# A decoder layer on one core: the second norm's modulation rows, two at a time inside attention

## The chip, the core and the metric

The kernel runs on one NeuronCore of a Trainium2 chip. The core has five engines that run their own instruction streams and meet only at semaphores: TensorE (PE; its weight loads are PEld), VectorE (DVE), ScalarE (ACT), GpSimd (POOL) and SyncE (SP), which here only issues DMAs. The metric is the device time of one execution in microseconds.

## The reference, cut to what matters

```python
mod = silu(c) @ w_ada + b_ada                        # c: 1 x 1024, w_ada: 1024 x 6144
shift1, scale1, gate1, shift2, scale2, gate2 = split(mod, 6)
h    = rms_norm(x, norm1_g) * (1 + scale1) + shift1  # x: 512 x 1024
q, k, v, qi, ki, wi, u, g_attn, g_pool = split(h @ w_in)
attn = top-128 attention (8 heads of 64; the keys by an indexer from qi, ki, wi)
pool = pooled means of u, a 128 x 128 product per group, a scale
x    = x + gate1 * ((sigmoid(g_attn) * (attn @ w_attn_br)
                     + sigmoid(g_pool) * (pool @ w_pool_br)) @ w_out)
h2   = rms_norm(x, norm2_g) * (1 + scale2) + shift2
x    = x + gate2 * ((silu(a) * b) @ w_down)           # a, b: a causal conv of h2 @ w_up
```

The change is about `shift2` and `scale2`, parts 3 and 4 of `mod` (part 1 is `scale1`, part 2 `gate1`, part 5 `gate2`). They are used for the first time in the second norm, long after attention.

## The kernel before, in words

Activations lie with their channels on the 128 partitions and the 512 tokens along the free dimension. Every float32 product is made of three passes over rounded parts: ACT copies 128 x 1024 weights out of `stage` into `wsplit` as the high part (line 732), POOL subtracts to get the low part (line 650), and PE multiplies the high part with both parts of the activations (line 1471, 16 matmuls, "high products") and the low part with the high part of the activations (line 1480, 8 matmuls, "low products"). `wsplit` has three places; ACT prepares weights three units ahead of PE.

**Loads.** SP issues everything in one fixed order. A weight item goes to one of three places of `stage`; it is issued when POOL has made the last low part from what lay there (`load_item`, line 539). ACT waits for the item's semaphore before it copies, and whatever stands behind that copy in ACT's stream waits too.

**One part of `mod` on DVE and PE.** For parts 1 to 5, DVE multiplies eight rows of 128 x 1024 by one column of `silu(c)` each and adds them into an accumulator (`mod_row_of`: the first row line 1091, the other seven line 1094); each row reads the sum that the row before it left. PE then adds up the partitions with eight products whose output is one column each (`mod_columns`, line 1565, 16 matmul records), and DVE adds the bias (`mod_vector`, line 1108). For parts 3 and 4 the rows come in four loads of 1 MB each (`load_early`), into `ada_early`, with accumulators of their own (`macc_early`). DVE adds part 3 behind the first norm and part 4 between the q products; PE's column sums stand behind `squares(3)` and behind the pooling product `u1`, in the bank PT.

**Attention** is 32 steps and five more to drain, written out step by step for each engine (t is the step; a pair is an even step and the odd one after it). At an even t PE computes the scores of steps t and t+1 (line 1707), then at each t the transposes of step t-3 (line 1719), and one half of a filler product: at even t its high products, at odd t its low ones, and at odd t behind them the products with v (line 1741). The fillers are listed in `FILLERS`: gp2, gp3, pb0, pb1, gp4, gp5, pb2, pb3, gp6, gp7, pb4 to pb7, ga0 to ga3. They share two banks in turn, so a filler may start when the filler two before it has been drained: a gp by ACT's tanh (line 847), a pb by DVE (line 1331). In each step DVE adds the scores to the ALiBi terms and takes their maximum (line 1309), makes the bias (line 1313), and normalises the probabilities of the step before (line 1320). ACT makes the ALiBi terms (line 889), exponentiates (line 920), copies the transposed probabilities (line 928) and, after a filler's low half, calls `chunk(name)`: it waits for the filler's product, copies the high part of the weights three units on, and only then drains the bank:

```python
def pool_gate(m):
    chunk(("gp", m))
    me.did(act.activation(ypool[:, m, :], bank(("gp", m))[:, :], ACT.Tanh, scale=0.5), drained["act"])
```

So the copy of gp4's weights stands in ACT's stream right ahead of the tanh that drains gp3, and pb1, two fillers on from gp3, waits for that tanh.

Of the kernel before, what the change touches and what calls it, by code (L numbers as in the profile page):

```python
# [11 lines left out]
P = 128  # L12
# [201 lines left out]
def build_layer(nc, x, c, w_ada, b_ada, norm1_g, w_in, q_norm_g, k_norm_g, w_attn_br, w_pool_grp, pool_scale,  # L214
# [17 lines left out]
    with ExitStack() as ctx:  # L232
# [102 lines left out]
        ada_early = [arena(f"ada_early{n}", [P, 2, D], F32, (24, 36, 44, 52)[n]) for n in range(KD // 2)]  # L335
        macc_early = [arena(f"macc_early{n}", [P, D], F32, (16, 20)[n]) for n in range(2)]
# [18 lines left out]
        def column_bank(j):  # L355

            return {1: OB, 4: PT[1]}.get(j, PT[0])
# [7 lines left out]
        ada_early_in = [sem(f"ada_early_in{q}") for q in range(KD // 2)]  # L365
# [169 lines left out]
        def _(sp):  # L535
# [52 lines left out]
            def load_early(j, q):  # L588
                sp.wait_ge(mod_sum, KD if j == 3 else KD * ROW_TURN[3] + 2 * q + 2)
                if j == 3 and q == 0:  # L590
                    sp.wait_ge(mod_first, 1)
                sp.dma_start(ada_early[q][:, :, :], ada[:, 2 * q:2 * q + 2, j * D:(j + 1) * D]
                             ).then_inc(ada_early_in[q], 16)

            for n, item in enumerate(sch.items):
                if n == NSTAGE:
                    for q in range(KD // 2):
                        load_early(3, q)
                if n in (NSTAGE + 3, NSTAGE + 4):
                    for q in (2 * (n - NSTAGE - 3), 2 * (n - NSTAGE - 3) + 1):  # L600
                        load_early(4, q)
                if item[:3] == ("w", "up", (3 * P, FF + 3 * P)):
                    sp.wait_ge(x2_ok, 2 * NT)
                    sp.dma_start(gate_row[:, :], b_ada[0:1, 5 * D:6 * D].to_broadcast([P, D])).then_inc(gate_in, 16)
                    for q in range(KD // 2):
                        load_last(q)
                load_item(n)
            for n in range(2 * NT):
                half, t = divmod(n, NT)
                sp.wait_ge(out_ok, n + 1)  # L610
                sp.dma_start(out[0, t * P:(t + 1) * P, half * S:(half + 1) * S], ost[:, t, :]).then_inc(stored[t], 16)
# [435 lines left out]
        def _(dve):  # L1047
# [16 lines left out]
            def mod_row_of(j, k):  # L1064

                q, r = divmod(k, 2)
                if j == 1:
                    if r == 0:
                        dve.wait_ge(ada_in[q][j], 16)
                    elif q == KD // 2 - 1:  # L1070
                        dve.wait_ge(ada_end_in, 16)
                    row = ada_first[q][j][:, r, :]
                elif j in (3, 4):
                    if r == 0:
                        dve.wait_ge(ada_early_in[q], 16 * (j - 2))
                    row = ada_early[q][:, r, :]
                elif j == 2:
                    if r == 0:
                        dve.wait_ge(ada_mid_in[q % 2], 16 * (q // 2 + 1))
                    row = ada_mid[q % 2][:, r, :]  # L1080
                else:
                    if r == 0:
                        dve.wait_ge(ada_last_in[q], 16)
                    row = ada_last[q][:, r, :]
                acc = macc_early[j - 3] if j in (3, 4) else macc
                if k == 0:
                    if j == 2:
                        dve.wait_ge(used, sch.unit["mg", KA - 2] + 1)
                    if j == 5:
                        dve.wait_ge(gate_sum, 2)  # L1090
                    me.did(dve.tensor_scalar(acc[:, :], row, csil[:, 0:1], None, ALU.mult), mod_sum)
                else:
                    dve.wait_ge(mod_sum, KD * ROW_TURN[j] + k)
                    me.did(dve.scalar_tensor_tensor(out=acc[:, :], in0=row, scalar=csil[:, k:k + 1],  # L1094
                                                    in1=acc[:, :], op0=ALU.mult, op1=ALU.add), mod_sum)
# [74 lines left out]
            mod_rows(3, 0)  # L1170
            mod_rows(3, 1)
# [7 lines left out]
            mod_rows(3, 2)  # L1179
            mod_rows(3, 3)  # L1180
# [41 lines left out]
            for n in range(KA):  # L1222
# [9 lines left out]
                mod_rows(4, n)  # L1232
# [32 lines left out]
            mod_vector(3)  # L1265
            top_rounds(2)
            pool_mean(1)
            mod_vector(4)
# [65 lines left out]

            def merged_low(m):
# [5 lines left out]
            for m in range(KD):  # L1341
                if m:
                    merged_low(m - 1)
                if m in (2, 4):
# [119 lines left out]
        def _(pe):  # L1464
# [94 lines left out]
            def mod_columns(j):  # L1559
# [3 lines left out]
                acc = macc if j == 1 else macc_early[j - 3]  # L1563
# [5 lines left out]
            def gate_sums(j, n):  # L1569

                pe.wait_ge(mod_sum, KD * (ROW_TURN[j] + 1))
                for half in range(2):
# [68 lines left out]
            def v_turn(m):  # L1641
                pe.wait_ge(drained["act"], drained_count[sch.chunk["v", m]][1])
                if m < 2:
                    pe.wait_ge(mod_ok, ROW_TURN[3 + m] + 2)
# [20 lines left out]
            mod_columns(3)  # L1665
            for g in range(1, KA):
                product(("u", g), hT)
                if g == 1:
                    mod_columns(4)
# [24 lines left out]
            for t in range(SLOTS - 1):  # L1694
# [27 lines left out]
                if filler(t) and t < STEPS + 3:  # L1722
                    name, part = filler(t)
                    if part == "high":
                        await_bank(pe, name)
                    (high_products if part == "high" else low_products)(
                        sch.unit[name], bank(name), mix if name[0] == "pb" else hT)
                if t % 2 and 5 <= t < STEPS + 4:
# [8 lines left out]
                    if (t - 5) % (2 * NT) == 0 and m >= 2:  # L1737
                        pe.wait_ge(head_lo, m - 1)
                    for j in range(i + 1):
# [8 lines left out]
            for m in range(0, KD, 2):  # L1748
                for n in (m, m + 1):
                    product(("ab", n), qT)  # L1750
                if m + 4 < KD:
# [114 lines left out]
```

## Time and profile before

| | us |
|---|---|
| median of three runs | 754.99 (754.11 to 756.42) |
| the profiled execution, its own time | 759.15 |
| its span, first to last instruction | 757.2 |
| PE busy | 739.7 (98% of the span) |
| DVE, ACT, POOL busy | 379.0, 306.6, 312.3 |

PE is busy nearly everywhere; the first norm lies around 39 to 53 us, the u products start near 93 us, attention runs from about 187 to 298 us, the second norm lies near 360 to 400 us, and the MLP fills the rest.
### The profile page before, as it was taken

Reading aid. Unit: us, or ns where it says so; the run is one execution under the profiler, and the core shown is the slowest. Engines: PE = TensorE matmul, PEld = TensorE weight load, DVE = VectorE, ACT = ScalarE, POOL = GpSimd, SP = SyncE. Lnnn points to the kernel's source line nnn. Section 1 sums busy time; section 2 is a strip of 40 time slices with the busy share of each in tenths; the row PEclk is TensorE's granted clock in tenths of the full one; section 3 lists DMA queues with packets and bytes.
Section 4 is the critical chain, followed back from the end, with each engine's and each line's share of the span. In section 5 each row is a group of like instructions: output and inputs, shape, how many; then the busy total and the mean of one; then the engine's idle time right before and its main releaser. Section 6 shows DMA issues by size and latency. Waiting matters only on the chain.

```text
span 757.2 us, 9497 instructions
## 1 busy us (share of the span) xinstructions
PE 739.7 (98%) x3568; PEld 597.2 (79%) x3568; DVE 379.0 (50%) x693; ACT 306.6 (40%) x501; POOL 312.3 (41%) x165
## 2 busy tenths in 40 slices
PE   4989999999999999999999999999999999999997
PEld 3467788888777777887899888888788888888886
DVE  2588699972446551774685435464443433004002
ACT  4224513256756763334455343434334343212120
POOL 1125338562623332547423444444444444443431
PEclk9969989999999999999999999999999999999999
DMA  8995511221113113644338344323323321233301
GB/s 327 381 338 204 187 55 57 71 97 56 57 57 112 57 56 107 262 159 128 97 95 267 112 111 112 91 76 112 101 68 110 111 99 68 84 112 112 137 2 56
DMA packets 83995, 92.75 MB, mean 122 GB/s; under 512 B 2035, under 2 KB 66287, under 8 KB 83951
## 3 DMA queue, kind: packets, MB, share of 16 engines
q1 hardware_dynamic: 82719, 87.43, 35.6%
q10 hardware_dynamic: 1232, 4.72, 1.7%
q8 instruction: 29, 0.48, 0.3%
q14 instruction: 15, 0.12, 0.1%
HBM read 90.05 MB, written 2.10 MB: 122 GB/s over the span
## 4 chain that ended last, share of the span: by engine, by line
PE 96%; DVE 1%; DMA 1%; ACT 1%; SPq 0%; issue 0%; DVEq 0%; ACTq 0%
PE bank L1471 42%; PE bank L1491 21%; PE bank L1480 21%; PE bank L1547 2%; PE bank L1741 1%; PE bank L1719 1%; PE bank L1707 1%; PE bank L1513 1%; PE bank L1625 1%; DMA xtok<-in_x_dram 1%; PE bank L1565 1%; PE bank L1614 1%; ACT junk L747 1%; PE bank L1518 1%; PE bank L1775 1%; PE bank L1532 0%
## 5 line engine op out<-in xcount | busy, mean ns | idle before, releaser
L650 POOL TENSOR_TENSOR wsplit<-stage,wsplit 128x1024 fp32r<-128x1024 f32 (+1 forms) x120 | 275.0, 2295 | 395.2 <-ACT wsplit L732 391.7
L1471 PE MATMUL bank<-hT,wsplit 128*128 128x512 f32 (+1 forms) x1264 | 295.3, 386 | 0.0
L1471 PEld LDWEIGHTS bank<-hT,wsplit 128*128 128x128 f32 x1264 | 231.8, 190 | 46.5 <-issue 0.9
L732 ACT ACTIVATE wsplit<-stage 128x1024 fp32r<-128x1024 f32 (+1 forms) x120 | 119.8, 1000 | 280.9 <-PE bank L1480 196.7
L1480 PE MATMUL bank<-hT,wsplit 128*128 128x512 f32 (+1 forms) x632 | 152.8, 384 | 0.0
L1480 PEld LDWEIGHTS bank<-hT,wsplit 128*128 128x128 f32 x632 | 114.7, 188 | 23.5 <-issue 0.8
L1491 PE MATMUL bank<-wsplit,guT 128*128 128x512 f32 x528 | 119.8, 389 | 0.0
L1491 PEld LDWEIGHTS bank<-wsplit,guT 128*128 128x128 f32 x528 | 99.1, 188 | 20.5
L1429 DVE SCALAR_TENSOR_TENSOR yb<-bank,conv,yb 128x511 f32<-128x511 f32 (+1 forms) x44 | 32.9, 749 | 65.1 <-ACT yb L1022 64.3
L1429 DVE SCALAR_TENSOR_TENSOR ya<-bank,conv,ya 128x511 f32<-128x511 f32 (+1 forms) x44 | 33.0, 749 | 59.2 <-ACT ya L1022 58.4
L1364 DVE TENSOR_TENSOR tmp_last<-bank,gate_row 128x512 f32<-128x512 f32 x8 | 5.5, 688 | 101.7 <-PE bank L1491 101.7
L1309 DVE CUSTOM_DVE_ANT_0 logit<-logit,bank 128x128 f32<-128x128 f32 (+3 forms) x32 | 15.4, 483 | 39.3 <-PE bank L1707 36.2
L920 ACT ACTIVATE prob<-logit,sbias,stat 128x128 f32<-128x128 f32 (+3 forms) x32 | 20.9, 653 | 26.7 <-DVE sbias L1313 19.4
L1218 DVE MATCH_REPLACE8 work<-top,work 128x256 f32<-128x256 f32 (+2 forms) x45 | 24.0, 542 | 0.0
L1491 PE MATMUL bank<-wsplit,merged 128*128 128x512 f32 x96 | 22.5, 394 | 0.0
L1491 PE MATMUL bank<-own,merged 128*128 128x512 f32 x96 | 22.5, 391 | 0.0
L1215 DVE MAX8 top<-work 128x8 f32<-128x256 f32 (+2 forms) x45 | 22.2, 549 | 0.5
L1094 DVE SCALAR_TENSOR_TENSOR macc_early<-ada_early,csil,macc_early 128x1024 f32<-128x1024 f32 x14 | 22.1, 1575 | 0.5
L1491 PEld LDWEIGHTS bank<-wsplit,merged 128*128 128x128 f32 x96 | 18.0, 188 | 4.2 <-issue 0.5
L1320 DVE TENSOR_SCALAR prob<-prob,sinv 128x128 f32<-128x128 f32 (+3 forms) x32 | 20.4, 639 | 1.1
L1491 PEld LDWEIGHTS bank<-own,merged 128*128 128x128 f32 x96 | 17.9, 188 | 3.6
L1174 DVE TENSOR_TENSOR guT<-ya,guT 128x512 fp32r<-128x512 f32 x22 | 19.3, 875 | 0.7 <-ACT guT L1028 0.7
(188 smaller groups left out, 731.8 us busy)
## 6 DMA issues: line engine op xcount, KB each, us to landing
stage<-in_w_up_dram SPq DMA_DIRECT2D x44, 512.0 KB, 5.2
stage<-in_w_in_dram SPq DMA_DIRECT2D x17, 1024.0 KB, 5.3
stage<-in_w_down_dram SPq DMA_DIRECT2D x10, 1024.0 KB, 5.0
ada_early<-in_w_ada_dram SPq DMA_DIRECT2D x8, 1024.0 KB, 10.1
ada<-in_w_ada_dram SPq DMA_DIRECT2D x7, 1024.0 KB, 11.7
ada_mid<-in_w_ada_dram ACTq DMA_DIRECT2D x4, 1024.0 KB, 8.1
stage<-in_w_out_dram SPq DMA_DIRECT2D x4, 1024.0 KB, 6.1
ada_last<-in_w_ada_dram SPq DMA_DIRECT2D x4, 1024.0 KB, 11.1
```

Of the source, the lines that this page charges most:

```text
L650: pool.tensor_tensor(unit_split(n, 1), unit_source(n), unit_split(n, 0).bitcast(F32), ALU.subtract).then_inc(low, 1)
L732: me.did(act.activation(unit_split(n, 0), unit_source(n), ACT.Copy), high)
L920: me.did(act.activation(prob[:, t % 3, 0:n], logit[:, t % 2, 0:n], ACT.Exp, bias=sbias[:, t:t + 1], scale=stat[:, 2, r:r + 1], accum_out=s ...
L1094: me.did(dve.scalar_tensor_tensor(out=acc[:, :], in0=row, scalar=csil[:, k:k + 1], in1=acc[:, :], op0=ALU.mult, op1=ALU.add), mod_sum)
L1174: me.did(dve.tensor_tensor(out_ap, full, hi.bitcast(F32), ALU.subtract), signal)
L1215: found = [me.did(dve.max(top8[:, i, :], row_of(src, i))) for i in range(1, NT)]
L1218: me.did(dve.match_replace(out=row_of(work, i), in_to_replace=top8[:, i, :], in_values=row_of(src, i), imm_value=TAKEN))
L1320: me.did(dve.tensor_scalar(prob[:, (t - 1) % 3, 0:n], prob[:, (t - 1) % 3, 0:n], sinv[:, t - 1:t], None, ALU.mult), prob_ok)
L1429: me.did(dve.scalar_tensor_tensor(out=y[:, m % 2, back:], in0=bank((kind, m))[:, 0:S - back], scalar=w, in1=y[:, m % 2, back:], op0=ALU.mu ...
L1471: pe.matmul(out_bank[:, tokens], hi[:, k, :], rhs[:, part, k, tokens], start=k == 0 and part == 0, stop=False)
L1480: mm = pe.matmul(out_bank[:, tokens], lo[:, k, :], rhs[:, 0, k, tokens], start=False, stop=k == nk - 1)
L1491: mm = pe.matmul(out_bank[:, :], rows_of[:, a, k0 + r, t * P:(t + 1) * P], unit_split(n, b)[:, r, :], start=first and r == 0 and (a, b) == ...
```

## The change

The rows of parts 3 and 4 are no longer loaded as four loads of two rows but as sixteen loads of one row (0.5 MB) each, into two buffers `ada_row` in turn. They are issued by SP behind the eight weight items from gp2's on, two behind each. Row r waits (from r = 2) until DVE has added row r-2. DVE adds one row at the end of each odd step: part 3 in steps 1 to 15, part 4 in steps 21 to 35, into the common accumulator `macc`. PE's column sums of part 3 stand behind the high products of step 18 and those of part 4 behind the products ab0 and ab1 after attention, all in the bank OB. The waits for `mod_ok` move with them.

```diff
-        ada_early = [arena(f"ada_early{n}", [P, 2, D], F32, (24, 36, 44, 52)[n]) for n in range(KD // 2)]
-        macc_early = [arena(f"macc_early{n}", [P, D], F32, (16, 20)[n]) for n in range(2)]
+        ada_row = [arena(f"ada_row{n}", [P, D], F32, (40, 44)[n]) for n in range(2)]
...
-            def load_early(j, q):
-                sp.wait_ge(mod_sum, KD if j == 3 else KD * ROW_TURN[3] + 2 * q + 2)
-                if j == 3 and q == 0:
-                    sp.wait_ge(mod_first, 1)
-                sp.dma_start(ada_early[q][:, :, :], ada[:, 2 * q:2 * q + 2, j * D:(j + 1) * D]
-                             ).then_inc(ada_early_in[q], 16)
-
+            def load_row(r):
+
+                if r >= 2:
+                    sp.wait_ge(mod_sum, KD * ROW_TURN[3] + r - 1)
+                j, k = 3 + r // KD, r % KD
+                sp.dma_start(ada_row[r % 2][:, :], ada[:, k, j * D:(j + 1) * D]).then_inc(ada_row_in[r % 2], 16)
+
+            rows_after = sorted({sch.item_of[sch.unit[name]] for name in FILLERS})
+            rows_after.append(rows_after[-1] + 1)
             for n, item in enumerate(sch.items):
-                if n == NSTAGE:
-                    for q in range(KD // 2):
-                        load_early(3, q)
-                if n in (NSTAGE + 3, NSTAGE + 4):
-                    for q in (2 * (n - NSTAGE - 3), 2 * (n - NSTAGE - 3) + 1):
-                        load_early(4, q)
...
                 load_item(n)
+                if n in rows_after:
+                    i = rows_after.index(n)
+                    load_row(2 * i)
+                    load_row(2 * i + 1)
...
-            mod_rows(3, 0)
-            mod_rows(3, 1)
...
-            mod_rows(3, 2)
-            mod_rows(3, 3)
...
-                mod_rows(4, n)
...
-            mod_vector(3)
...
-            mod_vector(4)
...
+                if t % 2 and t < 2 * KD:
+                    mod_row_of(3, t // 2)
+                if t == 19:
+                    mod_vector(3)
+                if t % 2 and 20 <= t < 20 + 2 * KD:
+                    mod_row_of(4, (t - 20) // 2)
...
+                if m == 2:
+                    mod_vector(4)
...
-                if m < 2:
-                    pe.wait_ge(mod_ok, ROW_TURN[3 + m] + 2)
...
-            mod_columns(3)
...
-                if g == 1:
-                    mod_columns(4)
...
+                if t == 18:
+                    mod_columns(3)
...
+                    if t - 5 == 4 * NT:
+                        pe.wait_ge(mod_ok, ROW_TURN[3] + 2)
...
+                if m == 0:
+                    mod_columns(4)
```

SP's queue from the fourth weight item on, before (`stage` are the weight items; the last run of five ends with gp2's, then come pb0's from `w_pool_br`, and gp4's and gp6's from `w_in`):

```order
L549 DMA stage<-in_w_in_dram 128x8x256 [waits low]
L592 DMA ada_early_134<-in_w_ada_dram 128x2x1024 [waits mod_sum]
L592 DMA ada_early_135<-in_w_ada_dram 128x2x1024 [waits mod_sum]
L549 DMA stage<-in_w_in_dram 128x8x256 [waits low] x5
L549 DMA stage<-in_w_pool_br_dram 128x4x512 [waits low]
L549 DMA stage<-in_w_in_dram 128x8x256 [waits low] x2
L549 DMA stage<-in_w_pool_br_dram 128x4x512 [waits low]
L549 DMA stage<-in_w_in_dram 128x8x256 [waits low] x2
```

And in the changed kernel, from the nine waiting items that end with gp2's:

```order
L548 DMA stage<-in_w_in_dram 128x8x256 [waits low] x9
L592 DMA ada_row_132<-in_w_ada_dram 128x1024
L592 DMA ada_row_133<-in_w_ada_dram 128x1024
L548 DMA stage<-in_w_pool_br_dram 128x4x512 [waits low]
L592 DMA ada_row_132<-in_w_ada_dram 128x1024 [waits mod_sum]
L592 DMA ada_row_133<-in_w_ada_dram 128x1024 [waits mod_sum]
L548 DMA stage<-in_w_in_dram 128x8x256 [waits low]
L592 DMA ada_row_132<-in_w_ada_dram 128x1024 [waits mod_sum]
L592 DMA ada_row_133<-in_w_ada_dram 128x1024 [waits mod_sum]
L548 DMA stage<-in_w_in_dram 128x8x256 [waits low]
```

The early loads are gone, and gp4's item now stands behind two rows that wait for DVE's sums.

PE around the first column sums before (`squares` is the row with output 128x2, the column sums are the rows with 128x1):

```order
L1471 MATMUL bank<-hT,wsplit 128x512 x16
L1480 MATMUL bank<-hT,wsplit 128x512 x8
L1625 MATMUL bank<-halves,sq 128x2 x4
L1565 MATMUL bank<-ones,macc_early_136 128x1 x8
L1471 MATMUL bank<-hT,wsplit 128x512 x16
L1480 MATMUL bank<-hT,wsplit 128x512 x8
L1565 MATMUL bank<-ones,macc_early_137 128x1 x8
L1471 MATMUL bank<-hT,wsplit 128x512 x16
L1480 MATMUL bank<-hT,wsplit 128x512 x8
```

In the changed kernel the same place reads

```order
L1474 MATMUL bank<-hT,wsplit 128x512 x16
L1483 MATMUL bank<-hT,wsplit 128x512 x8
L1630 MATMUL bank<-halves,sq 128x2 x4
L1474 MATMUL bank<-hT,wsplit 128x512 x16
L1483 MATMUL bank<-hT,wsplit 128x512 x8
L1474 MATMUL bank<-hT,wsplit 128x512 x16
```

so that only `squares` is left between two dense products. The sums of part 3 stand in attention, at step 18:

```order
L1707 MATMUL bank<-kT,qT 128x512 x6
L1719 MATMUL bank<-ident,prob 128x128 x3
L1474 MATMUL bank<-hT,wsplit 128x512 x16
L1568 MATMUL bank<-ones,macc 128x1 x8
L1719 MATMUL bank<-ident,prob 128x128
L1483 MATMUL bank<-hT,wsplit 128x512 x8
L1745 MATMUL bank<-pT,vS 64x128 x6
```

They lie between the filler's high and low products. DVE in steps 3 and 4 of attention before (`logit` 128x512 is step 3's, `prob` the step before it):

```order
L1309 ISA logit,smax<-logit,bank 128x512
L1309 ISA smax 128x1
L1313 TENSOR_SCALAR sbias<-smax,stat 128x1
L1318 RECIPROCAL sinv<-ssum 128x1
L1320 TENSOR_SCALAR prob<-prob,sinv 128x512
L1309 ISA logit,smax<-logit,bank 128x256
```

and now:

```order
L1303 ISA logit,smax<-logit,bank 128x512
L1303 ISA smax 128x1
L1307 TENSOR_SCALAR sbias<-smax,stat 128x1
L1312 RECIPROCAL sinv<-ssum 128x1
L1314 TENSOR_SCALAR prob<-prob,sinv 128x512
L1095 SCALAR_TENSOR_TENSOR macc<-ada_row_133,csil,macc 128x1024
L1303 ISA logit,smax<-logit,bank 128x256
```

The added row stands between step 3's last instruction and step 4's first.

## Rows read from the trace of the kernel before

**Rows 1.** The page: span, and busy time, share and instructions of each engine.

```profile
span 757.2 us, 9497 instructions
...
PE 739.7 (98%) x3568; PEld 597.2 (79%) x3568; DVE 379.0 (50%) x693; ACT 306.6 (40%) x501; POOL 312.3 (41%) x165
```

**Rows 2.** The waits of TensorE: engine, line, releaser, total us, times, longest.

```profile
PE bank L1532 <- DMA xtok<-in_x_dram: 5.7, 1, 5.7
PE bank L1525 <- POOL dsel L638: 3.3, 1, 3.3
PE bank L1513 <- ACT hT L765: 2.1, 1, 2.1
PE bank L1513 <- DVE hT L1142: 1.3, 1, 1.3
PE bank L1532 <- ACT xT L753: 1.1, 1, 1.1
```

**Rows 3.** Timeline of TensorE, 96 to 113 us: start, us, engine, line, operation, idle before.

```profile
98.43 0.95 PE L1625 MATMUL bank<-halves,sq 128*128 128x2 f32 x8
99.24 2.29 PE L1565 MATMUL bank<-ones,macc_early 128*128 128x1 f32 x16
101.39 6.72 PE L1471 MATMUL bank<-hT,wsplit 128*128 128x512 f32 x16
...
109.80 1.84 PE L1565 MATMUL bank<-ones,macc_early 128*128 128x1 f32 x16
111.50 3.93 PE L1471 MATMUL bank<-hT,wsplit 128*128 128x512 f32 x16
```

**Rows 4.** Windows of 1 us: busy times of the engines, then granted clock, DMA share, GB/s.

```profile
100.00:101.00 1.00, 1.00 (x10) 1.00 (x9) 1.00 (x4) 0.31 (x1) 1.00 (x1) 0.82 0.00 0
101.00:102.00 1.00, 1.00 (x5) 0.90 (x6) 1.00 (x5) 0.00 (x0) 1.00 (x1) 0.50 0.00 0
106.00:107.00 1.00, 1.00 (x4) 0.80 (x3) 1.00 (x3) 0.00 (x0) 0.00 (x0) 0.50 0.64 215
```

**Rows 5.** Timeline of SyncE's queue, 140 to 180 us.

```profile
175.83 0.37 SPq L549 DMA_DIRECT2D stage<-in_w_in_dram  x1
```

**Rows 6.** Transfers issued between 220 and 232 us: size, us from issue to landing.

```profile
stage<-in_w_pool_br_dram SPq DMA_DIRECT2D x1, 1024.0 KB, 5.2
stage<-in_w_in_dram SPq DMA_DIRECT2D x1, 1024.0 KB, 7.7
```

**Rows 7.** Timeline of all engines, 194 to 206 us.

```profile
194.01 5.08 POOL L650 TENSOR_TENSOR wsplit<-stage,wsplit 128x1024 fp32r<-128x1024 f32 x3
...
197.45 0.50 DVE L1320 TENSOR_SCALAR prob<-prob,sinv 128x512 f32<-128x512 f32 x1
...
201.17 0.42 DVE L1309 CUSTOM_DVE_ANT_0 logit<-logit,bank 128x256 f32<-128x256 f32 x1 [3.22 <-PE bank L1707]
...
202.64 1.05 ACT L732 ACTIVATE wsplit<-stage 128x1024 fp32r<-128x1024 f32 x1
...
203.59 0.58 ACT L847 ACTIVATE ypool<-bank 128x512 f32<-128x512 f32 x1
...
204.44 0.44 PE L1741 MATMUL bank<-pT,vS 128*64 128x128 f32 x4
...
205.94 2.09 PE L1471 MATMUL bank<-mix,wsplit 128*128 128x512 f32 x8
```

**Rows 8.** One line of VectorE, 53 to 70 us: durations ns min/median/max of the early rows.

```profile
L1094 DVE SCALAR_TENSOR_TENSOR macc_early<-ada_early,csil,macc_early x7: 1283/1285/3360, 53.7 to 68.7; 128x1024 f32<-128x1024 f32 x7
```

**Rows 9.** Timeline of VectorE, 255 to 272 us, where pairs are shortest.

```profile
260.38 0.29 DVE L1309 CUSTOM_DVE_ANT_0 logit<-logit,bank 128x128 f32<-128x128 f32 x1 [0.85 <-PE bank L1707]
...
265.33 0.69 DVE L1309 CUSTOM_DVE_ANT_0 logit<-logit,bank 128x512 f32<-128x512 f32 x1 [2.43 <-PE bank L1707]
...
270.05 0.42 DVE L1309 CUSTOM_DVE_ANT_0 logit<-logit,bank 128x256 f32<-128x256 f32 x1 [1.35 <-PE bank L1707]
```

**Rows 10.** Timeline of GpSimd, 255 to 272 us.

```profile
262.85 2.39 POOL L650 TENSOR_TENSOR wsplit<-stage,wsplit 128x1024 fp32r<-128x1024 f32 x1 [3.53 <-ACT wsplit L732]
```

More of the change, by code:

```diff
@@ L355, in column_bank @@
         def column_bank(j):
-            return {1: OB, 4: PT[1]}.get(j, PT[0])
+            return OB
         def sem(name):
@@ L364, in build_layer @@
         wgrp_in = sem("wgrp_in")
-        ada_early_in = [sem(f"ada_early_in{q}") for q in range(KD // 2)]
+        ada_row_in = [sem(f"ada_row_in{n}") for n in range(2)]
         ada_mid_in = [sem(f"ada_mid_in{n}") for n in range(2)]
@@ L1073, in mod_row_of @@
                 elif j in (3, 4):
-                    if r == 0:
-                        dve.wait_ge(ada_early_in[q], 16 * (j - 2))
-                    row = ada_early[q][:, r, :]
+                    n = KD * (j - 3) + k
+                    dve.wait_ge(ada_row_in[n % 2], 16 * (n // 2 + 1))
+                    row = ada_row[n % 2][:, :]
                 elif j == 2:
@@ L1084, in mod_row_of @@
                     row = ada_last[q][:, r, :]
-                acc = macc_early[j - 3] if j in (3, 4) else macc
+                acc = macc
                 if k == 0:
-                    if j == 2:
+                    if j == 3:
                         dve.wait_ge(used, sch.unit["mg", KA - 2] + 1)
+                    if j in (4, 2):
+                        dve.wait_ge(mod_col, ROW_TURN[j])
                     if j == 5:
@@ L1562, in mod_columns @@
                     pe.wait_ge(vecs, 1)
-                acc = macc if j == 1 else macc_early[j - 3]
+                acc = macc
                 for k in range(KD):
@@ L1571, in gate_sums @@
                 pe.wait_ge(mod_sum, KD * (ROW_TURN[j] + 1))
+                if n == 0:
+                    pe.wait_ge(mod_ok, ROW_TURN[4] + 2)
                 for half in range(2):
```

## The prediction

> **What bounds the kernel now.** I read the page first: PE is busy for 739.7 of 757.2 us [rows 1]. Then its waits: there are five, 13.5 us in all, the last two in the products of the first norm [rows 2]. From there to the end PE never waits for anybody. So work taken from DVE or from the early transfers gives nothing by itself, and three things only can move the end: how much PE has to do, the clock at which it does it, and a wait that appears where none was.
>
> Next I read PE's timeline where the column sums stand. From 98.43 us `squares` and the first column sums keep PE for 3.0 us with outputs one or two columns wide. The 16 dense matmuls behind them take 6.72 us; the same 16 at 111.50 take 3.93, and the column sums themselves 2.29 against 1.84 [rows 3]. The windows say why: the granted clock falls within the window 100 to 101 (0.82), is 0.50, which is 1.2 GHz, in the next, and still 0.50 at 106 to 107 [rows 4]. The second column sums, 1.84 us alone between dense products, are followed by no such fall [rows 3]. **The fall at 101 us costs (6.72 - 3.93) + (2.29 - 1.84) = 3.2 us.**
>
> **What goes.** Fourteen additions and two first rows leave DVE between 53 and 100 us, and 8 MB of loads leave that stretch. PE waited for neither, so this is 0. `mod_columns(3)` leaves its place behind `squares`, which then stands alone between dense products with 0.95 us, shorter than the 1.84 us that did no harm [rows 3]. I take the fall to go with it: **-3.2 us**, with 0 as the other end, if `squares` is enough or if the undisturbed runs never had it (the profiled execution took 759.15, the median of the runs is 754.99, and I can't tell whether part of the 4.2 us is this fall).
>
> **What moves on PE.** Both column sums are only moved, 1.84 us each at the full clock [rows 3]: 0 in sum. Their sums are ready in time: part 3's last row is added at step 15 and wanted at step 18, part 4's at step 35 and wanted two products after attention. The new waits on `mod_ok`, before the products with v of step 21 and before the gate's sums, come a pair or more after what they wait for: 0. At step 18 the sums and one transpose leave PE without dense products for a little over the harmless 1.84 us and well under the 3.0 that did harm; I take 0 and keep 3.2 as the other end.
>
> **What moves on DVE.** A row takes 1.28 us, the median of the early ones, and up to 3.36 where POOL is at work [rows 8]. One row per pair goes where DVE waits for the next scores: 3.22 us at 201.17 [rows 7], but only 0.85, 2.43 and 1.35 us in the short pairs with pb fillers [rows 9]. There the row makes DVE late by about 0.4 us at 260.38, and the next normalisation can then fall behind POOL's 2.39 us at 262.85 [rows 10]. But the three gaps together are 4.6 us and three rows 3.8, so DVE is back in time before the pairs grow long again. I take 0.3 us, from 0 to 2.1, which is 3.36 - 1.28.
>
> The Trainium skill (SBUF — State Buffer, Who interferes with whom) says that a DVE instruction with two inputs in SBUF and a GpSimd one that reads SBUF exclude each other, the second waiting until the first is done. The added rows are of that kind, and the maximum of 3.36 us agrees.
>
> **What moves on SP: the step that decides.** SP issues in order. Before, gp4's weights were issued at 175.83, right when their place came free, 27 us ahead of use [rows 5]. Now they stand behind row 3 (the fourth row), which waits until DVE has added row 1, at the end of step 3. In the trace DVE ends step 3 at 197.45 + 0.50 = 197.95 [rows 7]. A row of 1.28 us behind it ends at 199.2, or at 200.4 if it has to wait for POOL's chain that ends at 199.1 [rows 7, 8]. Then row 3 is issued (0.5 MB) and 0.4 us later, an issue taking 0.37 [rows 5], gp4's item (1 MB). Of two items of 1 MB issued 0.4 us apart the first landed after 5.2 us and the second after 7.7 [rows 6]: 1 MB ahead adds 2.5, so 0.5 MB adds 1.25, and gp4 lands some 6.5 us after its issue: at 206.1 to 207.3, say 206.7.
>
> ACT copies gp4's weights at 202.64, in step 4 [rows 7]. It will stand there for some 4 us. Behind it in ACT's stream is the tanh that drains gp3's bank; in the trace it ends at 203.59 + 0.58 = 204.17, 1.53 us after the copy began. PE needs that bank for pb1 at 205.94 [rows 7]. So there was 1.8 us of cover, and the load is late by 4.1: 206.7 + 1.5 = 208.2, **a wait of 2.3 us on PE** (1.7 to 2.9). Behind it ACT must still make two steps' ALiBi terms, exponentials and copies before PE's products with v of step 7; by the durations in this stretch that is another 0.3 us. In the gp pairs that follow everybody catches up. Sum: **+2.6 us**, bounds 1.7 and 3.2. The later items have more room: each has four steps or more between the row that holds it back and its copy.
>
> By the rule of the skill named above, row 1 would wait for POOL's whole chain if the chain had begun first; then the load lands at 207.3 and the wait is 2.9 instead of 2.3 us.
>
> **The clock again.** This wait doesn't stand in dense work. From 204.44 PE does products with v, scores and transposes; dense matmuls begin at 205.94 [rows 7]. With the wait that is 1.5 + 2.3 = 3.8 us without them, 2.3 of it idle, against 3.0 us of narrow work before the fall at 101 us [rows 3, 4]. I expect a second fall. It would cost at most what the first did, 3.2 us, and less where PE does small matmuls: **+2.7 us**, with 0 as the lower end.
>
> **The sum.** 759.15 - 3.2 + 2.6 + 2.7 + 0.3 = 761.6 for an execution like the profiled one, 2.4 us more. I carry the difference over to the median: 754.99 + 2.4 = **757.4 us**. About 0.3% (2.3 us) is what a measurement of this kernel can tell from no change, so this lies just at that bound.
>
> **Rivals.**
>
> *A wait without a second fall of the clock.* All as above, but TensorE keeps its clock: -3.2 + 2.6 + 0.3 = -0.3, 754.7 us. For it: the 1.84 us at 109.80 and the 1.5 us from 204.44 without dense products were followed by no fall [rows 3, 7]. Against it: neither is half as long as the 3.8 us.
>
> *No gain to set against it.* The fall at 101 us is absent from the plain runs or stays with `squares` alone. Then with the new wait and its fall +5.6, 760.6 us; with the wait alone +2.9, 757.9.
>
> *Faster: gp4's weights come in time.* If the item lands by about 204.4, ACT's tanh ends before 205.94 and PE waits for nothing. This decides it: 2.3 us earlier than I reckon. The row on DVE would have to end earlier, or 1.5 MB to land in some 5 us. What remains is the early gain: -3.2 + 0.3 = -2.9, 752.1 us. Against it speaks the 7.7 us row [rows 6].
>
> *DVE becomes the bound in the pb pairs.* A row there that meets POOL costs up to 3.36 us [rows 8] where DVE has a gap of 0.85 [rows 9]: DVE would be 2.5 us late for the next scores, and what PE doesn't cover of that adds to any case, up to 2 us.
>
> **Chances.** The forecast 0.33 (757.4); wait without fall 0.24 (754.7); no early gain with wait and fall 0.19 (760.6), with the wait alone 0.12 (757.9); weights in time 0.12 (752.1 with the early gain, 755.3 without). A range from 752.5 to 761.0 leaves out most of the last and the tails. Faster by over 0.3% needs less than 752.7: 0.13. Slower by over 0.3% needs more than 757.3: a good half of the forecast, most of 760.6, half of 757.9, together 0.44. Within: 0.43.
>
> **What would show it.** In the trace after: a wait of PE at pb1's high products of about 2.3 us, released by ACT's tanh; ACT idle for some 4 us before its copy of gp4's weights, released by a transfer; gp4's item issued right behind row 3, some 25 us later than before against the same step. The clock at full between 90 and 110 us with 3.7 to 3.9 us for the 16 products behind `squares`; 0.50 for some windows behind pb1. If PE has no new wait in steps 4 to 7, the step on SP is wrong, and with it the forecast; if the clock stays up there, the second term is; if the clock still falls near 100 us, the first is. PE waiting for logits or probabilities in steps 22 to 29 would show that I priced DVE's rows too low.

## The result

| | before | after |
|---|---|---|
| median, first comparison (6 runs each) | 755.70 (754.11 to 758.38) | 760.60 (759.86 to 761.51) |
| ratio to before | | 1.0063 [1.0042, 1.0083] |
| median, second comparison | 756.44 (17 runs, 754.09 to 759.25) | 761.12 (6 runs, 760.00 to 762.11) |
| ratio to before | | 1.0062 [1.0049, 1.0076] |
| profiled execution, span, mean granted clock | 759.15, 757.2, 0.986 | 760.37, 758.6, 0.991 |

Times are in microseconds. The changed kernel is slower by 0.63%. 757.4 was forecast, 752.5 to 761.0 as the range; the case that came is the rival called "no gain to set against it" with wait and fall, priced at 760.6.

The page of after, span and engines (for [rows 1]):

```profile
span 758.6 us, 9512 instructions
...
PE 734.9 (97%) x3568; PEld 592.2 (78%) x3568; DVE 380.5 (50%) x693; ACT 306.7 (40%) x501; POOL 317.6 (42%) x165
```

PE is busy for 4.8 us less than in [rows 1], and yet the span is longer: the profiled execution of before ran at half clock for longer, after waits for longer. Its waits of TensorE, in the form of [rows 2]:

```profile
PE bank L1535 <- DMA xtok<-in_x_dram: 6.4, 1, 6.4
...
PE bank L1474 <- ACT ypool L846: 3.0, 1, 3.0
...
PE bank L1745 <- ACT pT L927: 0.4, 1, 0.4
```

Two of these are new: 3.0 us for ACT's tanh at L846, and 0.4 us for a copy of transposed probabilities. The others stand before 55 us, up to the first norm, and they differ from one execution to the next. PE's timeline at the places of [rows 3] and of the end of [rows 7]:

```profile
97.67 0.95 PE L1630 MATMUL bank<-halves,sq 128*128 128x2 f32 x8
98.48 3.93 PE L1474 MATMUL bank<-hT,wsplit 128*128 128x512 f32 x16
...
197.91 0.66 PE L1719 MATMUL bank<-ident,prob 128*128 128x128 f32 x4
201.58 3.62 PE L1474 MATMUL bank<-mix,wsplit 128*128 128x512 f32 x8 [3.01 <-ACT ypool L846]
...
207.38 0.55 PE L1707 MATMUL bank<-kT,qT 64*128 64x128 f32 x6
```

The 16 products behind `squares` take 3.93 us: the fall at 101 us is gone. But pb1's 8 high products, 2.09 us in [rows 7], take 3.62 behind the wait. The windows of after (the granted clock is the third number from the end):

```profile
101.00:102.00 1.00, 1.00 (x6) 0.83 (x5) 1.00 (x5) 0.00 (x0) 0.92 (x3) 1.00 0.00 0
...
200.00:201.00 1.00, 0.00 (x0) 0.00 (x0) 0.00 (x0) 1.00 (x2) 0.00 (x0) 1.00 0.52 213
201.00:202.00 1.00, 0.42 (x1) 0.34 (x2) 0.00 (x0) 1.00 (x4) 0.88 (x1) 0.89 0.04 16
202.00:203.00 1.00, 1.00 (x4) 0.79 (x3) 0.87 (x5) 1.00 (x5) 1.00 (x1) 0.50 0.00 0
...
204.00:205.00 1.00, 1.00 (x4) 0.60 (x3) 0.96 (x5) 1.00 (x4) 0.00 (x0) 0.50 0.02 8
205.00:206.00 1.00, 1.00 (x6) 0.89 (x5) 0.96 (x3) 1.00 (x3) 0.20 (x1) 0.90 0.00 0
```

Where [rows 4] had 0.50 at 101 to 102, here stands 1.00. The clock is at 1.2 GHz for 3.4 us behind the wait instead. The chain behind that wait. First SyncE's queue:

```profile
185.80 7.61 SPq L592 DMA_DIRECT2D ada_row<-in_w_ada_dram  x2
193.45 0.43 SPq L548 DMA_DIRECT2D stage<-in_w_in_dram  x1
```

GpSimd and VectorE, from the timeline of all engines:

```profile
186.87 5.10 POOL L649 TENSOR_TENSOR wsplit<-stage,wsplit 128x1024 fp32r<-128x1024 f32 x3
...
190.74 2.32 DVE L1095 SCALAR_TENSOR_TENSOR macc<-ada_row,csil,macc 128x1024 f32<-128x1024 f32 x1
```

And ScalarE:

```profile
194.87 0.26 ACT L927 ACTIVATE pT<-bank 128x128 f32<-128x128 f32 x1
199.99 1.06 ACT L731 ACTIVATE wsplit<-stage 128x1024 fp32r<-128x1024 f32 x1 [4.86 <-issue]
200.95 0.58 ACT L846 ACTIVATE ypool<-bank 128x512 f32<-128x512 f32 x1
```

Read it from the top. SP stands with the two rows until DVE has added row 1. That addition begins at 190.74, while POOL is inside its chain, and ends at 193.06. Then row 3 and gp4's item go out; the item was issued at 175.83 in [rows 5]. It lands 6.5 us later, at 199.95. ACT has done nothing for 4.86 us (the profile calls it "issue", since it can't name the transfer), copies at 199.99, and the tanh ends at 201.53. PE starts at 201.58.

### The profile page after: what moved, and what is told of

Read it like the earlier page. It is cut to its first block, busy times and chain, and to the rows that moved or that the text cites. A ratio compares the mean times of both kernels' runs of the same rounds, so it can differ in the third digit from the quotient of the medians.

```text
span 758.6 us, 9512 instructions
## 1 busy us (share of the span) xinstructions
PE 734.9 (97%) x3568; PEld 592.2 (78%) x3568; DVE 380.5 (50%) x693; ACT 306.7 (40%) x501; POOL 317.6 (42%) x165
## 4 chain that ended last, share of the span: by engine, by line
PE 93%; DMA 2%; SPq 2%; DVE 2%; issue 1%; ACT 0%; DVEq 0%; ACTq 0%
PE bank L1474 42%; PE bank L1494 21%; PE bank L1483 21%; DMA ada<-in_w_ada_dram 2%; PE bank L1745 1%; PE bank L1719 1%; PE bank L1707 1%; SPq L558 1%; PE bank L1516 1%; PE bank L1630 1%; PE bank L1568 1%; PE bank L1619 1%; DVE hT L1143 1%; PE bank L1521 1%; PE bank L1781 1%
## 5 line engine op out<-in xcount | busy, mean ns | idle before, releaser
L649 POOL TENSOR_TENSOR wsplit<-stage,wsplit 128x1024 fp32r<-128x1024 f32 (+1 forms) x120 | 279.9, 2336 | 390.8 <-ACT wsplit L731 388.7
L1314 DVE TENSOR_SCALAR prob<-prob,sinv 128x128 f32<-128x128 f32 (+3 forms) x32 | 23.0, 719 | 1.1
L1474 PE MATMUL bank<-mix,wsplit 128*128 128x512 f32 x64 | 18.3, 431 | 3.0 <-ACT ypool L846 3.0
L1095 DVE SCALAR_TENSOR_TENSOR macc<-ada_row,csil,macc 128x1024 f32<-128x1024 f32 x14 | 21.1, 1506 | 0.1
```

The lines of the kernel that those rows point to most:

```text
L649: pool.tensor_tensor(unit_split(n, 1), unit_source(n), unit_split(n, 0).bitcast(F32), ALU.subtract).then_inc(low, 1)
L1314: me.did(dve.tensor_scalar(prob[:, (t - 1) % 3, 0:n], prob[:, (t - 1) % 3, 0:n], sinv[:, t - 1:t], None, ALU.mult), prob_ok)
L1474: pe.matmul(out_bank[:, tokens], hi[:, k, :], rhs[:, part, k, tokens], start=k == 0 and part == 0, stop=False)
```

## The experiments

Four questions: does the late item alone make the loss; what did the early fall of the clock cost before; do the moved rows and column sums cost anything themselves; how does the loss go with the length of the wait. The measured medians, with the ratio to the kernel before run beside them on the same chip:

| run | median us (runs) | ratio to before |
|---|---|---|
| a1_gp4_first | 755.55 (12) | 0.9993 [0.9978, 1.0007] |
| a2_gp4_before_row3 | 758.79 (6) | 1.0034 [1.0022, 1.0047] |
| a4_row_at_step10 | 755.72 (12) | 0.9990 [0.9977, 1.0002] |
| a5_sums18_twice | 759.86 (6) | 1.0044 [1.0031, 1.0057] |
| a6_row_at_step12 | 755.24 (12) | 0.9992 [0.9978, 1.0007] |
| b1_columns_apart | 755.06 (12) | 0.9986 [0.9974, 0.9999] |
| b6_columns_apart_again | 754.67 (12) | 0.9982 [0.9967, 0.9996] |
| b2_gp4_late | 761.16 (4) | 1.0070 [1.0044, 1.0096] |
| b3_columns_twice | 761.02 (5) | 1.0060 [1.0038, 1.0083] |
| b5_gp4_less_late | 756.11 (12) | 1.0005 [0.9992, 1.0017] |

The kernel before is not one number. Of 70 runs of it beside these, 24 took 753.7 to 755.4 us with a mean clock of 0.992 or 0.993, and 46 took 756.0 to 759.4 with 0.986 to 0.991; none lies between. Traces tell the groups apart only in part: of the 24 runs of the version with the column sums apart, further down, three lie above 756.0 us too, one of them the profiled 756.27, whose trace has no fall near 100 us. Since before's median moves with the mix, a second measure is used as well: in each profiled execution, the time from the start of `squares(3)` to the end of the span. It leaves out the start of the kernel, which varies by 2 us (`squares(3)` starts between 96.8 and 98.9 us, in no order that follows the change).

| profiled execution | from `squares(3)` to the end |
|---|---|
| b1 / b6 (columns apart) | 655.6 / 655.6 |
| a6 (row at step 12) | 655.6 |
| a1 / a4 (gp4 first) | 656.0 / 656.1 |
| b5 (gp4 less late) | 656.6 |
| before | 658.8 |
| a5 (sums of step 18 twice) | 659.4 |
| a2 (gp4 before row 3) | 660.1 |
| after / the same once more | 660.9 / 661.5 |
| b2 (gp4 late) / b3 (columns twice) | 661.7 / 662.2 |

**gp4's item first.** From the changed kernel: rows 2 to 5 go out behind gp4's item.

```diff
                 load_item(n)
-                if n in rows_after:
-                    i = rows_after.index(n)
+                pairs = {rows_after[0]: (0,), rows_after[1]: (), rows_after[2]: (1, 2)}
+                for i in pairs.get(n, (rows_after.index(n),) if n in rows_after else ()):
                     load_row(2 * i)
                     load_row(2 * i + 1)
```

> The changed kernel, with one thing undone: rows 2 to 5 are issued behind gp4's item, so the item is issued when its place comes free, as before the change. All sixteen rows are still added in attention and the column sums stay where the change put them. Theory (the late load makes the wait, and the wait makes the clock fall): no wait of PE at pb1's high products, the clock at full from 200 to 206 us, and the 4.9 us between 755.7 and 760.6 are gone: 755.0 to 756.5 us. Rival (DVE's rows in attention, or the moved column sums, cost the time themselves): 758 us or more, with waits of PE for logits or probabilities, or the wait comes back at a later filler. If the early fall of the clock were in the plain runs of before, the kernel would come out 3 us below before, at about 752.5.

PE's timeline at pb1, and where it still waits, in the pair of steps 14 and 15:

```profile
197.32 0.66 PE L1719 MATMUL bank<-ident,prob 128*128 128x128 f32 x4
197.73 2.09 PE L1474 MATMUL bank<-mix,wsplit 128*128 128x512 f32 x8
...
201.92 0.55 PE L1707 MATMUL bank<-kT,qT 64*128 64x128 f32 x6
...
226.15 1.09 PE L1745 MATMUL bank<-pT,vS 128*64 128x128 f32 x16 [0.40 <-ACT pT L927]
```

No wait, 2.09 us for the 8 products, and 4.19 us from pb1's start to the next scores, where after takes 5.80. With all sixteen rows still in attention, the time is 755.55. The 752.5 named for an early fall in all of before's runs did not come. So two rows of 0.5 MB ahead of one item in SP's queue are the loss against before: 5.0 us between 755.55 and the 760.60 of the first comparison. Of this, 4.9 us are seen in the profiled executions (656.0 against 660.9); the 0.4 us that is left at the last row shown comes back below.

**The same wait put into the kernel before.** No row is moved; SP holds gp4's item for a semaphore of step 4.

```diff
+                if n == sch.item_of[sch.unit["gp", 4]]:
+                    sp.wait_ge(bias_ok, 5)
                 load_item(n)
```

> The kernel before, with gp4's weight item held back until DVE has made the biases of attention's step 4, which puts its landing at about 207 us, as late as in the changed kernel; no row is moved. Theory (the late load alone makes the loss): PE waits 2.5 to 3.5 us at pb1's high products for ACT's tanh, the clock falls to 0.50 behind it for some 3.5 us (1.5 us lost), and the run is 4 to 5.5 us slower than before. Rival (the wait is only part, the moved DVE rows make the rest): 2 to 3 us slower. Rival (the clock fell in the changed kernel for another reason than the wait): the wait stands there, but the high half behind it takes 2.1 us.

SP's queue, and PE's timeline at the early column sums and at pb1:

```profile
199.45 1.19 SPq L549 DMA_DIRECT2D stage<-in_w_in_dram  x2
```

```profile
98.44 1.93 PE L1567 MATMUL bank<-ones,macc_early 128*128 128x1 f32 x16
100.23 5.49 PE L1473 MATMUL bank<-hT,wsplit 128*128 128x512 f32 x16
...
206.37 3.63 PE L1473 MATMUL bank<-mix,wsplit 128*128 128x512 f32 x8 [2.61 <-ACT ypool L849]
```

The loss is there, +4.5 us between the medians, with the same two parts: 2.61 us of wait and 3.63 us for 8 products. The rows are not needed for it. This execution also has the early fall, but a shorter one: 5.49 us for 16 products instead of the 6.72 of [rows 3].

**The early fall: column sums apart from `squares`, and column sums twice.** Both from the kernel before.

```diff
             squares(KA - 1)
-            mod_columns(3)
             for g in range(1, KA):
                 product(("u", g), hT)
-                if g == 1:
-                    mod_columns(4)
+                if g in (1, 2):
+                    mod_columns(g + 2)
```

> The kernel before, with the column sums of part 3 moved from behind squares(3) to behind the product u1 and those of part 4 from u1 to u2; nothing else. Theory A (the fall of the clock at 101 us goes with the pair squares plus column sums, and is in most plain runs): about 3 us faster, 752.5 us. Theory B (the fall was in the profiled execution and in few plain runs): the median stays at 755 to 756 us, at most 0.5 us lower, and the profiled execution has the clock at full between 95 and 115 us with 3.7 to 3.95 us for each high half.

```diff
-                for k in range(KD):
+                for _ in range(2 if j == 3 else 1):
+                    for k in range(KD):
```

> The kernel before, with the column sums of part 3 computed twice in a row behind squares(3), into the same bank: the stretch of PE with outputs one or two columns wide grows from 3.0 to some 4.8 us. By its work alone it costs 1.84 us. Theory B (the fall of the clock is a matter of chance for a stretch of 3.0 us): with the longer stretch it comes in most or all runs, and the cost is 1.84 + 3.2 = 5 us, or more with the column sums themselves at half clock. Theory A (the fall was in all runs before already): only 1.9 to 2.8 us slower. If the fall had nothing to do with this stretch: 1.84 us slower, with the clock at full in the profile.

PE's timeline with the sums apart, and then with the sums twice:

```profile
98.76 0.95 PE L1625 MATMUL bank<-halves,sq 128*128 128x2 f32 x8
99.57 3.93 PE L1471 MATMUL bank<-hT,wsplit 128*128 128x512 f32 x16
...
105.16 1.84 PE L1565 MATMUL bank<-ones,macc_early 128*128 128x1 f32 x16
106.86 3.93 PE L1471 MATMUL bank<-hT,wsplit 128*128 128x512 f32 x16
```

```profile
97.24 0.95 PE L1626 MATMUL bank<-halves,sq 128*128 128x2 f32 x8
98.05 5.67 PE L1566 MATMUL bank<-ones,macc_early 128*128 128x1 f32 x32
103.58 6.75 PE L1471 MATMUL bank<-hT,wsplit 128*128 128x512 f32 x16
```

Apart, each does no harm, and the part of before's runs above 757 us is gone: with a second set, further down, 24 runs lie between 754.05 and 756.43. The median of the first set, 755.06, is 1.6 us below before's 756.64 on the same chip (the ratio says 1.0), where theory A wanted 3 and theory B at most 0.5, so neither came whole. Twice in a row, the profiled execution loses 2.0 us in the sums themselves (5.67 against 2 x 1.84) and 2.8 us in the products. The median is 6.0 us above the version with the sums apart, of which 1.84 is work. The fall is not in every run of before. The shortest one seen costs 1.6 us, the fastest run with the sums apart took 754.05, and 24 runs of before took 755.41 or less, which is less than the sum of the two. Where it is, it has not always the same length. Theory B's "few plain runs" was wrong, though: 46 of 70 runs are in the slower group. That is an upper count, since three of the 24 runs with the sums apart come to more than 756.0 us too, and no trace shows an execution of before that kept its clock.

**How much of the wait is DVE, how much transfer.** From the changed kernel: SP waits for row 1's sum, issues gp4's item, then row 3.

```diff
+                if n == rows_after[2]:
+                    sp.wait_ge(mod_sum, KD * ROW_TURN[3] + 2)
                 load_item(n)
+                if n == rows_after[2]:
+                    load_row(3)
...
-                    load_row(2 * i + 1)
+                    if i != 1:
+                        load_row(2 * i + 1)
```

> The changed kernel, with gp4's item issued between row 2 and row 3: SP still waits for DVE's sum of row 1 at the end of step 3, but only row 2 (0.5 MB) is ahead of the item in the transfers. Theory (the item is late by the wait for DVE and by 1.25 us of transfer for row 3, plus 0.4 us of issue): the wait of PE shrinks from 3.0 to some 1.4 us. If the clock falls with it as it did: 1.5 us lost there, sum about 3 us, 758.5 us. If 1.4 us of idle time and the 1.5 us of small products ahead of it are too little for a fall: 757 us. Rival (the wait for DVE alone makes the load late, the transfers share the engines so that row 3 costs the item nothing): the wait stays at 2.6 us or more, and the time at 760 us.

> The changed kernel itself, run again beside the others on one chip, since the kernel before spreads over 5 us from run to run. From the trace its loss against the order with gp4's item first is 3.0 us of wait and 1.5 us of half clock, so it should stay 4.5 to 5.3 us above that order (755.55 in the runs before), near 760.5 us, and spread over no more than 2 us.

SP's queue and PE's timeline with the item ahead of row 3, then PE's in the second execution of the changed kernel:

```profile
192.24 0.38 SPq L548 DMA_DIRECT2D stage<-in_w_in_dram  x1
192.66 12.70 SPq L592 DMA_DIRECT2D ada_row<-in_w_ada_dram  x3
```

```profile
199.90 2.87 PE L1479 MATMUL bank<-mix,wsplit 128*128 128x512 f32 x8 [2.18 <-ACT ypool L851]
...
205.69 0.55 PE L1712 MATMUL bank<-kT,qT 64*128 64x128 f32 x6
```

```profile
202.31 2.88 PE L1474 MATMUL bank<-mix,wsplit 128*128 128x512 f32 x8 [3.58 <-ACT ypool L846]
...
208.10 0.55 PE L1707 MATMUL bank<-kT,qT 64*128 64x128 f32 x6
```

The changed kernel run again took 761.12, 5.4 us above the order with gp4's item first beside it (with row 5 a step earlier, 755.72), where up to 5.3 was expected, and its six runs spread over 2.1 us. With the item ahead of row 3 the wait shrank to 2.18 us, not to the 1.4 expected. Against the same scores of step 4 the item goes out 0.36 us earlier and lands after 6.0 us instead of 6.5. Row 3 ahead of it costs it 0.9 us in all, where 1.65 had been reckoned: the rest is DVE's sum, which holds the item in either order. The clock falls again and costs the same. From pb1's start to the next scores it is 5.79 us here, 5.79 in the second execution of the changed kernel and 5.80 in the first, against 4.19 undisturbed: 1.6 us each time, behind waits of 2.2, 3.6 and 3.0 us.

**A shorter wait.** From the version with the sums apart: the item is held until ACT's first copy of transposed probabilities.

```diff
+                if n == sch.item_of[sch.unit["gp", 4]]:
+                    sp.wait_ge(pt_ok, 1)
                 load_item(n)
```

> The kernel before with the column sums apart, and besides gp4's item held back until ACT has copied the transposed probabilities of the first step, which should issue it some 2 us earlier than holding it for step 4's bias did (197.4 against 199.45 in that trace). The landing is then near 202.7, and with 1.8 us of cover PE's wait at pb1's high products is about 0.6 us instead of 2.6. Theory (the clock falls only with a longer stretch without dense products): 0.6 us for the wait and none for the clock, 755.7 us against 755.1 with the column sums apart alone. Rival (any wait there takes the clock down): 757.2 us, with 0.50 granted behind the wait.

> The kernel before with the column sums apart, once more, beside the other two on one chip: 755.0 us if its small gain over the kernel before (0.9986 in the runs before) holds, with no run above 757; 756 us or more if that gain was chance.

PE's timeline with the item less late:

```profile
202.82 2.12 PE L1473 MATMUL bank<-mix,wsplit 128*128 128x512 f32 x8 [0.62 <-ACT ypool L849]
...
207.10 0.55 PE L1708 MATMUL bank<-kT,qT 64*128 64x128 f32 x6
```

The wait is 0.62 us, as expected, and the clock keeps its level: 2.12 us for the 8 products and 4.28 to the scores. From `squares(3)` to the end it is 656.6 against 655.6, 1.0 us more. The medians differ by 1.4, where 0.6 was expected, and 0.4 of it has no name in this profile. Three of the 12 runs took 756.85 to 757.12 at a mean clock of 0.990, and no trace shows whether the clock fell there in those. The second set of the version with the sums apart took 754.67, none over 755.7. Its gain over before is small but twice measured: 0.9986 and 0.9982.

**What the rows cost.** From the order with gp4's item first, one row is added a step earlier. First row 5, then row 6:

```diff
-                if t % 2 and t < 2 * KD:
+                if t < 2 * KD and (t == 10 or t % 2 and t != 11):
                     mod_row_of(3, t // 2)
```

> The order with rows 2 to 5 behind gp4's item, and besides DVE adds row 5 at the end of step 10 instead of step 11. In the trace with gp4's item first the row at step 11 (1.27 us) stands between a normalisation that POOL draws out to 2.57 us and the scores of step 12; they come 1.2 us later, and PE waits 0.40 us for the copy of the transposed probabilities. Theory (this one row is all that the rows cost): ahead of the drawn-out normalisation the row is free, the wait of 0.40 us goes, and the time is 755.1 us. Rival (the row delays step 11's bias instead, and the wait moves): 755.5 us or more.

```diff
-                if t % 2 and t < 2 * KD:
+                if t < 2 * KD and (t == 12 or t % 2 and t != 13):
                     mod_row_of(3, t // 2)
```

> The order with rows 2 to 5 behind gp4's item, and besides DVE adds row 6 at the end of step 12 instead of step 13. The numbering of the run before this one was wrong: the row that stands behind the normalisation that POOL draws out to 2.57 us, ahead of the scores of step 14, is row 6 at the end of step 13. Theory (this row's 1.27 us behind the drawn-out normalisation is all that the rows cost): put ahead of it, the row is hidden by POOL's instruction, the wait of 0.40 us for the copy of the transposed probabilities goes, and the time is some 0.4 us less than with gp4's item first alone, 755.2 us. Rival (the row delays step 13's bias, and the wait stays or moves): 755.5 us or more.

VectorE's timeline of the order with gp4's item first, then of the last version:

```profile
220.30 2.57 DVE L1314 TENSOR_SCALAR prob<-prob,sinv 128x256 f32<-128x256 f32 x1
222.79 1.27 DVE L1095 SCALAR_TENSOR_TENSOR macc<-ada_row,csil,macc 128x1024 f32<-128x1024 f32 x1
```

```profile
221.36 1.28 DVE L1095 SCALAR_TENSOR_TENSOR macc<-ada_row,csil,macc 128x1024 f32<-128x1024 f32 x1
...
223.34 1.70 DVE L1314 TENSOR_SCALAR prob<-prob,sinv 128x256 f32<-128x256 f32 x1
```

Moving row 5 did nothing; I had counted the steps wrong, and PE's wait of 0.41 us stood where it was. Moving row 6 took that wait away. The normalisation meets POOL's subtraction (2.57 us where such a one takes 0.35 alone). A row behind it delays DVE's work on the scores of step 14 by its full 1.2 us. Ahead of it, the row uses mostly time that is lost anyway: the normalisation then takes 1.70 us, and DVE is late by some 0.3. From `squares(3)` to the end this version takes 655.6 us, the same as the version of before with the sums apart. So all other rows and both moved column sums cost nothing that this measure shows. The two medians on one chip, 755.24 and 754.67, leave up to about 1 us open: they differ by 0.6, and the runs of either spread over 2.2 and 1.6.

**Column sums in attention.** From the order with gp4's item first, part 3's sums at step 18 are computed twice, by the same edit as above.

> The order with rows 2 to 5 behind gp4's item, and besides the column sums of part 3 at step 18 are computed twice in a row: some 3.7 us with outputs one column wide in the middle of attention instead of 1.84. The work alone costs 1.8 us: 757.3 us. Theory (what was in the stretch behind squares(3), 3.0 us of narrow outputs, takes the clock down wherever it stands, in some executions or in all): the clock falls to 0.50 behind the sums and 1.5 to 3.2 us more are lost in most executions, 758.8 to 760.5 us. Rival (the place matters, attention's steady small products keep the clock): 757.3 us with the clock at full.

PE's timeline, and one window:

```profile
239.86 3.49 PE L1569 MATMUL bank<-ones,macc 128*128 128x1 f32 x30
...
243.27 3.57 PE L1483 MATMUL bank<-hT,wsplit 128*128 128x512 f32 x8
```

```profile
244.00:245.00 1.00, 1.00 (x4) 0.73 (x3) 0.00 (x0) 0.68 (x3) 0.00 (x0) 0.50 0.00 0
```

The 8 low products take 3.57 us instead of 2.07. The median is 4.1 us above that of the order with gp4's item first as it ran beside it (with row 5 a step earlier, 755.72), of which 1.84 is work; all six runs lie between 758.6 and 760.1. So the place gives no protection: once, for 1.84 us, part 3's sums do no harm at step 18, and twice they do.

## Why the prediction was right or wrong

**The early fall, -3.2: the size held, its use did not.** That the fall goes with `mod_columns(3)` behind `squares` was right: sums apart, sums twice and the profile of after all show it. But I subtracted 3.2 us from a median of three runs of which two (754.11 and 754.99) lie in the faster group; with 3.2 us taken off, either would lie 1.9 us or more below the fastest run of before, 753.72. Of the gap of 4.2 us between the profiled execution and the median, which I noted and set aside, 3.2 can be this. Over before's runs the term is worth 1.0 to 1.8 us: 1.0 and 1.4 by the two ratios, 1.8 by the medians of 70 and 24 runs (756.65, 754.86). Had the term been taken for what it was in those three runs, near zero, the forecast would have been the rival's 760.6.

**SP, +2.6: the mechanism was right in each step, the wait was under-sized.** The item behind row 3, ACT standing still, the tanh late and PE waiting at pb1 all came. PE starts pb1 3.3 us late (3.01 of wait as the profile counts it, the rest in how transposes and products overlap). My 2.6 was 2.3 of this wait and 0.3 for the products with v of step 7. PE doesn't wait at those in after, so the 0.3 did not come; the wait alone lies just above my upper bound of 3.2. What failed in it is the end of row 1 on DVE. I took 199.2 and 200.4 as its ends; on the time scale of the trace before, with the scores of step 4 at 200.40 there and at 192.78 in after, it ended at 200.7. The row ran into POOL's chain and took 2.32 us; I had charged it 1.28 and let it wait at most for a chain that ended at 199.1, where it ended at 199.6. Row 3 and the item followed at once, and the item landed at 207.6 on that scale, 0.9 us behind the 206.7 reckoned. The Trainium skill (SBUF — State Buffer, Who interferes with whom) says that the later of two such instructions waits until the first is done. This trace agrees: the row begins at 190.74, behind the last of POOL's three instructions (190.5), and ends 1.09 us after it, near its own 1.28. The transfer took 6.5 us, as reckoned.

**The second fall, +2.7: right that it comes, over-sized.** It lasted 3.4 us, not the 6.8 of the early one, and cost 1.6. I had scaled it from the only fall in the trace. The rival without it is refuted for this wait. In the profiled execution with a wait of 0.62 us TensorE does keep its clock.

**DVE, +0.3: right size, wrong place.** 0.4 us, at steps 14 and 15, behind a normalisation that POOL stretched, and not in the short pairs of steps 22 to 29 [rows 9, 10], where PE waited for nothing. The list of waits of the profiled runs shows no other.

**Column sums, moved: 0** was right, and so was taking no fall at step 18.

**The sum.** Measured on profiled executions: 3.3 + 1.6 + 0.4 = 5.3 us, and 660.9 - 655.6 = 5.3. The second execution has 5.9, its wait being longer. Less 1.0 to 1.8 for the early fall that before's runs mostly have, some 3.5 to 5 us are expected between medians; measured are 4.9 and 4.7. The forecast's 2.4 was too low by a term of SP 0.7 us too small and a gain 1.4 to 2.2 too large, which a second fall priced 1.1 us too high offset in part. That part is luck: with the second fall at its 1.6, the forecast would have been 1.1 us lower still.

## What to carry to other kernels

An in-order DMA queue ties every load behind a waiting one to that one's semaphore: before such a wait is put in, find the next load and reckon its landing from the latest end of the engine waited for, not its usual one; here two rows in another place of the queue gave back all 5 us. If the profiled execution is several us off the median of the plain runs, find out which of its features the plain runs share before subtracting one of them. Keep stretches of narrow matmuls on TensorE apart from each other: 1.84 us of them alone cost their own length here, and 3.0 us together up to 3.2 us more.

## What the runs showed of the hardware that was not expected

The same stretch of 3.0 us with outputs one or two columns wide took the clock to 0.50 in both profiled executions that have it, and by the times not in all runs: 24 of 70 are too fast for it, and at most 46 have it. Where it fell, the length differed: 6.8 us of half clock in the profiled execution of before (3.2 us lost), 3.4 us in the one with gp4's item late (1.6 us lost). With 5.7 us of sums behind `squares` it was about 10 us.

Behind PE's wait in attention the fall cost 1.6 us in each of four profiled executions, with waits of 2.2, 2.6, 3.0 and 3.6 us (5.79 or 5.80 us from pb1's start to the next scores, against 4.19), and none came with 0.62 in the one that was profiled. No run parts the idle time from the 1.5 us of small products ahead of it, so which of the two takes the clock down is not shown. It began within 2 us after the dense products' start, not in the idle time: in the windows of after the clock is 1.00 from 200 to 201, while PE does nothing, and 0.50 from 202 on, when it is busy again.

A VectorE normalisation of 128x256 elements took 2.57 us beside GpSimd's subtraction of 2.39 us, and 0.35 us a few instructions later. In the kernel before the same pair stands at 228.50 and 231.90 us, and PE had enough in hand to cover it; with a row behind it, it had not.
